# Weight products of two matmuls per block: all high products of a call first, then all low products

## The reference, cut to what matters

```
p = h @ w_in[l]
...
x = x + gt1 * mix
h = _rmsnorm(x, norm2_g[l]) * (1.0 + sc2) + sh2
x = x + gt2 * _conv_ffn(h, w_up[l], conv_w[l], conv_b[l], w_down[l])
```

## Time and profile before

| | |
|---|---|
| median of the timed runs | 2683.87 us |
| span of the profiled execution, first to last instruction | 2692.6 us |
| PE matmuls, share of the span | 97% |
| PE weight loads | 81% |
| VectorE (DVE) | 68% |
| ScalarE (ACT) | 47% |
| mean granted clock of TensorE | 0.991 |

### The profile page before, as it was taken

How to read it: one execution, slowest core, us unless ns; L and a number is a source line. 1 busy time by engine, 2 the same in 40 slices (tenths; PEclk the granted TensorE clock), 3 DMA queues, 4 the chain that set the end, 5 groups by cost and what they waited for, 6 DMA issues and landing times.

```text
span 2692.6 us, 48237 instructions
## 1 busy us (share of the span) xinstructions
PE 2619.7 (97%) x17788; PEld 2180.2 (81%) x17788; DVE 1835.1 (68%) x2686; ACT 1277.2 (47%) x1800; POOL 147.2 (5%) x148
## 2 busy tenths in 40 slices
PE   5999999999999999999999999999999999999998
PEld 1566666788888888888888888888888888888887
DVE  1465665778777777655567777777688888886554
ACT  2253334355555555444433356555555555554443
POOL 1311100120000000010000000000100000000000
PEclk8999999999999999999999999999999999999999
DMA  9977777345555555555545544455555555555553
GB/s 370 390 294 278 287 308 296 113 151 190 184 184 184 185 186 187 203 196 210 211 172 188 179 164 157 156 175 197 185 186 192 188 187 187 188 189 208 206 194 138
DMA packets 86806, 554.86 MB, mean 206 GB/s; under 512 B 8496, under 2 KB 8624, under 8 KB 24496
## 3 DMA queue, kind: packets, MB, share of 16 engines
q1 hardware_dynamic: 86272, 551.78, 55.9%
q10 hardware_dynamic: 432, 1.64, 0.2%
HBM read 551.29 MB, written 2.10 MB: 206 GB/s over the span
## 4 chain that ended last, share of the span: by engine, by line
PE 86%; DVE 4%; issue 4%; DMA 4%; ACT 1%; DVEq 0%; POOL 0%; SPq 0%; ACTq 0%; POOLq 0%
PE bank L630 38%; PE bank L631 19%; PE banks L630 15%; PE banks L631 8%; DMA raw<-in_stream_dram 4%; PE bank L679 2%; DVE wlo L1734 2%; DVE yb L2408 0%; DVE yb L2411 0%; PE banks L846 0%; PE banks L1211 0%; PE banks L1231 0%; ACT whi L1278 0%; PE banks L865 0%; PE banks L1220 0%
## 5 line engine op out<-in xcount | busy, mean ns | idle before, releaser
L1734 DVE TENSOR_TENSOR wlo<-raw,whi 128x1024 fp32r<-128x1024 f32 x846 | 1028.2, 1225 | 216.1 <-ACT whi L1278 211.6
L1278 ACT ACTIVATE whi<-raw 128x1024 fp32r<-128x1024 f32 x846 | 877.5, 1051 | 460.7 <-PE bank L631 327.9
L630 PE MATMUL bank<-act,whi 128*128 128x512 f32 x2928 | 1052.6, 402 | 4.4 <-ACT mix L1467 3.0
L631 PE MATMUL bank<-act,wlo 128*128 128x256 f32 x2928 | 821.1, 280 | 0.0
L630 PEld LDWEIGHTS bank<-act,whi 128*128 128x128 f32 x2928 | 549.8, 188 | 158.2 <-issue 20.1
L630 PE MATMUL banks<-act,whi 128*128 128x512 f32 x1792 | 636.6, 398 | 7.9 <-DVE act L1784 6.8
L631 PEld LDWEIGHTS bank<-act,wlo 128*128 128x128 f32 x2928 | 553.6, 189 | 0.7 <-issue 0.5
L631 PE MATMUL banks<-act,wlo 128*128 128x256 f32 x1792 | 504.6, 282 | 0.0
L630 PE MATMUL bank<-ff,whi 128*128 128x512 f32 x1408 | 493.3, 393 | 1.2 <-DVE wlo L1734 1.2
L630 PEld LDWEIGHTS banks<-act,whi 128*128 128x128 f32 x1792 | 338.7, 189 | 94.3 <-issue 12.7
L631 PE MATMUL bank<-ff,wlo 128*128 128x256 f32 x1408 | 392.9, 279 | 0.0
(11 more groups left out here) (277 smaller groups left out, 1898.2 us busy)
## 6 DMA issues: line engine op xcount, KB each, us to landing
raw<-in_stream_dram SPq DMA_DIRECT2D x519, 1024.0 KB, 4.8
x<-in_x_dram SPq DMA_DIRECT2D x1, 2048.0 KB, 13.8
lora_w<-in_lora_dram SPq DMA_DIRECT2D x1, 1536.0 KB, 14.3
pool_w<-in_pool_w_dram SPq DMA_DIRECT2D x1, 1024.0 KB, 12.1
out_dram<-x SPq DMA_DIRECT2D x2, 512.0 KB, 2.8
out_dram<-x ACTq DMA_DIRECT2D x2, 512.0 KB, 3.0
catt<-in_att_dram ACTq DMA_DIRECT2D x1, 576.0 KB, 3.4
par<-in_params_dram SPq DMA_DIRECT2D x1, 541.5 KB, 3.7
```

What stands on the lines that cost most here:

```text
L630: nc.tensor.matmul(tile_bank(t), wh, flat(pair[:, kt]), start=starts and n == 0, stop=False)
L631: mm = nc.tensor.matmul(small_half(t), wl, pair[:, kt, 0], start=False, stop=stops and last)
L1278: nc.scalar.activation(whi[:, k % RING], raw[:, r % RING, 8 * (k % 2):8 * (k % 2) + 8], ACT.Copy)\
L1734: nc.vector.tensor_tensor(wlo[:, k % RING], raw[:, r % RING, 8 * (k % 2):8 * (k % 2) + 8], whi[:, k % RING].bitcast(F32), ALU.subtract).th ...
```

## The change: the loop over the blocks is split in two

All high products of a call are issued first, in the order of the blocks, then all low products in the same order. The waits for activations stand before the high products as they did before. The first high product still opens the sum in the bank, and the last low product still closes it and carries the semaphore.

```
                     if ready is not None:
                         pe.wait_ge(a_ready, ready + kt + 1)
-                    wh, wl = whi[:, k % RING, b], wlo[:, k % RING, b]
+                    nc.tensor.matmul(tile_bank(t), whi[:, k % RING, b], flat(pair[:, kt]), start=starts and n == 0, stop=False)
+                for n, (b, kt) in enumerate(blocks):
                     last = n == len(blocks) - 1
-                    nc.tensor.matmul(tile_bank(t), wh, flat(pair[:, kt]), start=starts and n == 0, stop=False)
-                    mm = nc.tensor.matmul(small_half(t), wl, pair[:, kt, 0], start=False, stop=stops and last)
+                    mm = nc.tensor.matmul(small_half(t), wlo[:, k % RING, b], pair[:, kt, 0], start=False, stop=stops and last)
                 return mm
```

## The result

The changed kernel takes 2697.3 us (median of 8 runs, 2692.4 to 2699.2), beside 2684.5 us for the kernel before (8 runs, 2681.5 to 2694.4). The ratio is 1.0030, 95% interval 1.0016 to 1.0045: slower by 0.3%; the interval does not take in 1. The time lies within the range and within the likeliest case's own range (2662 to 2699), on the side that had 0.30.

What follows compares the result with a forecast made beforehand. The prediction took the start-to-start distance of PE's matmuls as the bound. 5434 steps of each kind times a bracket of 0 gave 0 us, so the forecast was the median, 2684 us, with a whole range of 2632 to 2730.

Steps and rivals of the forecast that it cites:

- likeliest case: Matmul steps on PE keep their lengths, with one pace or another: 0 us, own range 2662 to 2699 us; chance 0.74.
- the side that had 0.30: The changed kernel being slower than the kernel before, all cases taken together: chance 0.30.
- The bound: Start-to-start distance of matmuls on PE sets the time; matmuls cover 97% of the span.
- the waits: No added waits; in the mix product's second call the last high stays 0.47 us behind the last activation, costing nothing.
- The bracket: High-to-high less high-to-low, plus low-to-low less low-to-high, times 5434 steps: taken as 0, bounds -22.4 and +71 ns.
- the difference being zero, the forecast is the median: Final sum: 0 us on a 2692.6 us span, 8.7 us above the runs' median, so 2684 us.
- a new order may pick another pace: Over 5434 pairs, the fastest stretch's pace gives -22 us (2662), the slowest's +15 us (2699); slower had 0.19.
- The second rival: Weight loads pile up in the runs of lows: low-to-low +9 ns, +49 us, 2733 us; chance 0.11.
- The first rival: Alternating highs and lows has a price that runs drop: half the lower bound -61 us (2623), all 2562; chance 0.15.

Runs made afterwards that it cites:

- before_third: The kernel before, unchanged, profiled a third time; 2683.4 us.
- down_only: Against the kernel before, highs first, then lows, only in the calls of the two down products (operand ff2), all others by turns; ratio 1.0021.
- reset_each: Against the kernel before, by turns except halves with k a multiple of 8 (operand act2), which go highs first; 2700.9 us, ratio 1.0059.

## Why the prediction was right, and where it was off

**The bound and the waits** were right: the chain, the waits for `wlo` and the free places are as before. The mix product's second call starts its highs at 1850.89 and its lows at 1852.76 in the trace of after; the last activation was there at 1851.61 + 0.42 = 1852.03, half a microsecond ahead of the eighth high, as the working had it:

```profile
1850.89 2.03 PE L628 MATMUL bank<-gated,whi 128*128 128x512 f32 x8
1852.76 1.12 PE L631 MATMUL bank<-gated,wlo 128*128 128x256 f32 x8
...
1851.61 0.42 DVE L2416 TENSOR_TENSOR gated<-ft,gated 128x256 f32 x1 [0.57 <-ACT gated L1708]
```

**The bracket** came out near the forecast 0, but its reason held only for the highs. Forecast: high-to-high 230 to 236, low-to-low 117 to 120. Measured in the up and down products: 230.6 to 233.0 and 118.9 to 119.5. Against the profile of before, high-to-high less high-to-low is -1.7 ns and low-to-low less low-to-high +1.8 ns (means over all of each trace, steps with a wait or at the lower clock left out): +0.1 ns, under 1 us. Profile against profile 1.1 us was found. That the two cancel is luck: the -1.7 is there because the profile of before had the slow pace in the first up product. Against before_third they are -0.3 and +1.9, together 1.6 ns or 9 us. That a step holds the same in both orders is thus not enough: a low's step also depends on what stands ahead of it.

**The step that was off** is the last one: "the difference being zero, the forecast is the median". The difference was worked out against one execution of before, 10 us above the median, and it was zero only against that one. That execution had the slow pace in the first up product. Turns have several paces (346.7 or 353.3 ns with `act2`, 350 with `ff2` and `gated2`), and runs of eight have one for each operand: 349 with `act2`, 353 with `ff2`. Against an execution with the fast pace in the first up product, before_third, the change costs 12.1 us by the times of the profiled executions (2695.5 - 2683.4), and the table says where for 10 of them: up products +3.0 and +3.8, down products +2.1 each, input projection +1.1, mix +0.8, gates -0.9, convolution branch -1.5, recurrent mixer -0.5; most of the rest lies ahead of the table's first phase. The text had said that a new order may pick another pace, and gave this 0.19 of the chance; the size, +12.8 us, is in that case's range (+15 at most). That bound was made from paces of turns, though, and what came are the paces of runs, which no row of before showed; that they lie within it is luck too.

**The second rival came true in part**, though it had only 0.11. In a run of lows with `act2` the step grows from 113 to 120 ns, above the 118 from which it was to decide, and half the load takes this away. The term was mis-sized: 3 ns over the 116.7 of turns in the fast pace, not 9. It is also what the up products lose against that pace. A call's lows take 113 + 119 + 6 x 120 = 952 ns instead of 8 x 116.7 = 934, its highs 1842 instead of 8 x 230 = 1840: 20 ns a call, 2.5 ns a pair, 349.2 instead of 346.7. The argument against it, that a low beside a load already takes place by turns, set aside what the rival itself had said: by turns each second load has a whole high step to itself. The Trainium skill's page "TensorE: Matmul & The Clock Gate", section "LDWEIGHTS (loading the stationary operand)", puts a load at its columns over 1.2 GHz, an estimate of 107 ns for 128; the runs show a floor of 111 to 112.

**The first rival** (turns have a price, runs at 216 and 112) did not come: the highs of a run end at 227 ns, and of its lows only the first, with 113, comes near 112. The gap of 216 and 109 ns, worked out from the formula that the same page gives in its section "Back-to-back issue gap", is not reached by the mean step of any order here. The page gives that formula for a matmul by itself and says that weight loads count too in a stream, so the prediction's "whatever stands beside" is more than it states.

**Open:** why the down products lose 3.0 ns a pair (2.1 us over 704 pairs; high-to-high 233.0 and low-to-low 119.5, beside 231.8 to 232.5 and 117.6 to 118.2 by turns), since half the load changes little there; and what a pace is. That it outlasts hundreds of microseconds, differs between executions of one program, and can be changed by a single grouped call is shown; which part of the chip holds the state is not.

## What to carry to other kernels

Where PE is never idle, the time hangs on the step from one matmul's start to the next, and single nanoseconds of it count by the thousand; compare start distances stage by stage, not busy shares. Before carrying a difference over to the median, ask whether the profiled execution is a usual one: when its time is off the median, profile it again and see which stage moves. Where short matmuls are little longer than their weight loads, try them beside long ones: with `act2` here a low took 116.7 ns by turns at the fast pace and 120 in a row.

## What the runs showed of the hardware that was not expected

- By turns, in long stretches, pairs of 512 and 256 float32r columns step in one of three paces, 346.7, 350.0 or 353.3 ns, at a granted clock of 1.00 in the stretches of the earlier trace rows. Within the slowest, in the first up product of before, the steps repeat every three pairs (241, 120, 235, 114, 232, 118 ns); within the fastest all pairs are alike in the second up product of before (230, 117), and two kinds take turns in the first of down_only (230 and 113, 232 and 118).
- One run of eight highs and eight lows can change the pace of the turns behind it: from 346.6 to 353.3 ns in the first up product of reset_each. The slow pace then holds for the phase in both up products, where the second one had 346 to 347 in each execution of before.
- In a row of matmuls that each have their own load of 128 columns, the step is 111 to 112 ns with 128 columns to stream, and 120 with 256; with half the load and 256 columns it is 113 (`act2`). With 512 columns halving the load changes the step by +0.6 (`act2`) and -2.2 ns (`ff2`, calls of eight).
